# Which expert blocks' results stay on chip for the combining product: the last two, or the last one

## The reference

```
s     = sigmoid(h @ w_router)                     # 16 experts in 4 groups
idx   = top 2 experts of the best group           # by s + router_bias
gates = s[idx] / sum(s[idx])
act   = silu(h @ w_gate[e]) * (h @ w_up[e]) * gates[e]
y     = sum over e of act @ w_down[e]
x     = x + g2 * y
```

## Time and profile before

| | |
|---|---|
| median of three runs | 1651.51 us |
| the profiled execution | 1663.96 us |
| its span, first to last instruction | 1662.2 us |
| TensorE matmuls busy | 1446.6 us (87% of the span) |
| VectorE, ScalarE, GpSimd busy | 545.1, 372.3, 196.9 us |
| chain that ended last | TensorE 67%, DMA 12%, VectorE 8%, issue 5%, ScalarE 3% |
| granted TensorE clock, mean | 0.951 |
| DMA | 428.68 MB, 258 GB/s over the span |

### The profile page before, as it was taken

How to read it: one execution, slowest core, us unless ns; L and a number is a source line. 1 busy time by engine, 2 the same in 40 slices (tenths; PEclk the granted TensorE clock), 3 DMA queues, 4 the chain that set the end, 5 groups by cost and what they waited for, 6 DMA issues and landing times.

```text
span 1662.2 us, 26392 instructions
## 1 busy us (share of the span) xinstructions
PE 1446.6 (87%) x10704; PEld 857.0 (52%) x10704; DVE 545.1 (33%) x1329; ACT 372.3 (22%) x985; POOL 196.9 (12%) x286
## 2 busy tenths in 40 slices
PE   3989997998897998898989999979889899969982
PEld 1866674332676686332464456743327566843321
DVE  0126523211526625111522343332115257242114
ACT  1105421111212612111120342301102036121110
POOL 0100021101113022000110000210011000220011
PEclk9989998999999999999989999999989999979996
DMA  9996235999869126999958224379996940539992
GB/s 339 349 318 230 88 116 211 408 420 415 282 231 324 23 105 230 373 420 422 345 183 263 36 77 177 102 293 416 421 411 201 310 159 2 203 121 406 421 379 87
DMA packets 125027, 428.68 MB, mean 258 GB/s; under 512 B 13099, under 2 KB 55038, under 8 KB 100326
## 3 DMA queue, kind: packets, MB, share of 16 engines
q1 hardware_dynamic: 96854, 350.32, 54.9%
q0 software_dynamic: 21104, 72.71, 12.7%
q10 hardware_dynamic: 6944, 3.91, 0.8%
HBM read 389.20 MB, written 40.26 MB: 258 GB/s over the span
## 4 chain that ended last, share of the span: by engine, by line
PE 67%; DMA 12%; DVE 8%; issue 5%; ACT 3%; POOL 2%; another core or an unknown queue 2%; SPq 1%; DVEq 0%; ACTq 0%; POOLq 0%
PE bank L1681 59%; DMA work<-in_moe_w_gate 5%; DMA ring<-in_w_mod 4%; PE bank L1851 3%; DMA h_slots<-xn,row_of 2%; PE bank L2015 2%; ACT pp L1022 2%; PE bank L1738 1%; POOL small L698 1%; POOL h_slots L801 1%; DVE xn L1169 1%; DMA hT<-h_slots 1%; PE bank L1898 1%; SPq L606 1%
## 5 line engine op out<-in xcount | busy, mean ns | idle before, releaser
L1681 PE MATMUL bank<-ring,pp 128*32 128x512 f32 x2312 | 317.4, 597 | 14.0 <-issue 11.9
L1681 PE MATMUL bank<-ring,hT 128*128 128x256 f32 (+3 forms) x1142 | 272.2, 398 | 5.9 <-issue 3.3
L1681 PEld LDWEIGHTS bank<-ring,hT 128*128 128x128 f32 x1142 | 213.6, 196 | 62.7 <-issue 32.1
L1681 PE MATMUL bank<-work,pp 128*32 128x512 f32 x888 | 241.9, 628 | 3.0 <-DVE pp L1555 2.3
L1681 PE MATMUL bank<-ring,xn 128*128 128x256 f32 x768 | 168.2, 380 | 0.0
L1681 PEld LDWEIGHTS bank<-ring,pp 128*32 128x32 f32 x2312 | 87.4, 110 | 135.5 <-issue 134.5
L1681 PEld LDWEIGHTS bank<-ring,xn 128*128 128x128 f32 x768 | 145.0, 190 | 19.4
L1681 PE MATMUL bank<-V,pp 128*32 128x512 f32 x640 | 124.3, 634 | 30.5 <-issue 21.3
L1571 DVE TENSOR_TENSOR pp<-bank,pp 128x256 f32<-128x256 f32 x40 | 17.0, 425 | 340.1 <-ACT pp L1099 340.1
L1681 PE MATMUL bank<-ring,condT 128*32 128x256 f32 x1536 | 99.0, 404 | 17.0 <-DMA ring<-in_w_mod 17.0
L1022 ACT ACTIVATE pp<-bank,neg_max 128x384 f32<-128x384 f32 x192 | 96.7, 524 | 13.2 <-DVE neg_max L1462 10.1
(11 more groups left out here) (254 smaller groups left out, 1561.2 us busy)
## 6 DMA issues: line engine op xcount, KB each, us to landing
ring<-in_w_mod SPq DMA_DIRECT2D x96, 1024.0 KB, 8.2
ring<-in_moe_w_down SPq DMA_DIRECT2D x52, 1024.0 KB, 19.0
ring<-in_moe_w_gate SPq DMA_DIRECT2D x32, 1024.0 KB, 15.1
ring<-in_moe_w_up SPq DMA_DIRECT2D x32, 1024.0 KB, 17.5
hT<-h_slots POOLq DMA_DIRECT2D x36, 512.0 KB, 11.4
V<-in_moe_w_gate SPq DMA_DIRECT2D x16, 1024.0 KB, 13.9
V<-in_moe_w_up SPq DMA_DIRECT2D x16, 1024.0 KB, 16.3
work<-in_moe_w_gate SPq DMA_DIRECT2D x16, 1024.0 KB, 10.0
```

Source lines behind the costliest of these rows:

```text
L1681: return pe.matmul(out, lhsT, rhs, start=start, stop=stop)
```

## The change

`LATE` goes from 2 to 1. Block 8 is now stored and gathered like the eight before it, and only block 9's results are multiplied with the weighted matrix. `STORED` becomes 9, which changes the bound of the indirect loads and the weights that use it. The matrix has three squares of 128x128 instead of six, so it is turned in one go in block 4 (`LATE_PARTS` = 1), and the waits on `late_turned` and `lateT_ready` count by that. The semaphores of the stores count unevenly by parity now (five even blocks, four odd ones).

```diff
--- before.py
+++ after.py
@@ -32,7 +32,8 @@
 STARTS = [sum(SIZES[:i]) for i in range(E)]
 SLOTS = sum(SIZES)
 BLOCKS = SLOTS // P
-LATE = 2
+LATE = 1
+LATE_PARTS = -(-NB * LATE // 4)
 STORED = BLOCKS - LATE
 FURTHER = NT - NARROW
 PASSES = -(-FURTHER // P)
@@ -809,7 +810,8 @@
 
                 def stored_at(blk):
 
-                    return 16 * (STORED // 2 * L + blk // 2 + 1)
+                    each = (STORED + 1 - blk % 2) // 2
+                    return 16 * (each * L + blk // 2 + 1)
 
                 def block_out(blk):
                     pool.wait_ge(y_a, BLOCKS * L + blk + 2)
@@ -834,7 +836,7 @@
                     if blk == 2 and L < DEPTH - 1:
                         load_columns(L + 1, 0)
                 stored(STORED - 1)
-                pool.wait_ge(late_turned, 2 * (L + 1))
+                pool.wait_ge(late_turned, LATE_PARTS * (L + 1))
                 for b in range(NB):
                     for k, dst in enumerate((y_first, y_sum)):
                         nc.gpsimd.indirect_dma_start(dst[b], None, y_slots, rows_at(row_of[:, k, b:b + 1]),
@@ -1101,10 +1103,10 @@
                         turned_rows(n + 1, 1 - slot)
                     if blk > 0:
                         first_half(blk - 1)
-                    if blk in (4, 5):
+                    if 4 <= blk < 4 + LATE_PARTS:
                         i = 4 * (blk - 4)
                         w = min(4, NB * LATE - i)
-                        act.wait_ge(late_turned, 2 * L + blk - 3)
+                        act.wait_ge(late_turned, LATE_PARTS * L + blk - 3)
                         nc.scalar.copy(lateT[:, i:i + w, :], bank[3][:, 0:w * P].rearrange("p (i n) -> p i n", n=P))\
                             .then_inc(lateT_ready, 1)
                     turn_act(act, n, slot)
@@ -2097,7 +2099,7 @@
                         pe.wait_ge(late_ready, L + 1)
                         n = max(n for n in range(jobs["rank", L][0] + 1) if n % 4 == 3)
                         pe.wait_ge(freed[job_at[n][1]], job_at[n][2])
-                    pe.wait_ge(lateT_ready, 2 * L + i // 4)
+                    pe.wait_ge(lateT_ready, LATE_PARTS * L + i // 4)
                     for m in range(i, min(i + 4, NB * LATE)):
                         b, at = m // LATE, m % LATE * P
                         ins = pe.transpose(bank[3][:, (m - i) * P:(m - i + 1) * P], late[0][:, b, at:at + P], ident[:, :])
@@ -2106,13 +2108,13 @@
                 def turn_columns():
 
                     pe.wait_ge(mod_cols_in, 16 * (2 * (L + 1)))
-                    pe.wait_ge(lateT_ready, 2 * (L + 1))
+                    pe.wait_ge(lateT_ready, LATE_PARTS * (L + 1))
                     pe.transpose(bank[3][:, 256:288], m_in[:, 0, :], ident[0:32, 0:32]).then_inc(cols_turned, 1)
 
                 def add_late(b):
 
                     if b == 0:
-                        pe.wait_ge(lateT_ready, 2 * (L + 1))
+                        pe.wait_ge(lateT_ready, LATE_PARTS * (L + 1))
                         pe.wait_ge(cols_ready, min(L + 1, DEPTH - 1))
                         pe.wait_ge(act_full, BLOCKS * (L + 1) + 2)
                         pe.wait_ge(acT_ready, BLOCKS * (L + 1) + 1)
@@ -2133,10 +2135,8 @@
                         turn_rows(n + 1, 1 - slot, loaded(blk + 1))
                     if blk > 0:
                         block_down(blk - 1)
-                    if blk == 4:
-                        turn_late(0)
-                    if blk == 5:
-                        turn_late(4)
+                    if 4 <= blk < 4 + LATE_PARTS:
+                        turn_late(4 * (blk - 4))
                     if blk == 6 and L < DEPTH - 1:
                         turn_columns()
                     pe.wait_ge(act_full, n + 3)
```

## The result

The changed kernel takes 1696.77 us (median of four runs, 1694.87 to 1700.48) against 1653.72 us before (four runs, 1650.01 to 1658.09): a ratio of 1.0262, 95% interval 1.0228 to 1.0296. Slower by 43 us. The prediction was added to a median of 1651.51 us, from the three runs that stood then; a fourth of 1655.94 us moved that median up by 2.2 us. The profiled execution took 1697.12 us with a span of 1695.2 us. Against the one profile of the kernel before, whose span was 1662.2 us, that is only +33; why the two differences disagree turned out to be a finding of its own (run 9).

The account below looks back on a forecast made before the run. The prediction took two roads meeting at the first combining step as the bound, TensorE's slightly later, the gathered side with hardly any slack. 30.7 + 1.9 + 5.1 = +37.7 us on the median 1651.5 gave 1689 us, range 1670 to 1699.

Parts of the forecast that it names:

- the clock: Openings of layers 1 to 3: TensorE's stand lowers its granted clock, 2.3 + 0.5 + 2.3 = +5.1 us, between 0 and 7.
- The gate: End of each layer: block 8's store, issued only after block 8's copies, now gates all six indirect loads; the deciding term.
- The three terms of +30.7: Ends of layers 0 to 2: the next layer's scaling starts +9.9, +10.9 and +9.9 us later, together +30.7 us.
- Now two roads meet at L1166 almost together: First combining step, kernel before: block 9's copy and product against store, wait and indirect loads; TensorE's side slightly later.
- Layer 3: End of layer 3, no weights loading: store taken as 6 us, landing 5.0; +1.9 us, at the upper end +5.9.
- Removed products and turns: Six of twelve combining products a layer costed at nothing; three of six matrix turns at zero, at most 0.5 us a layer.
- Who else waits: SyncE's queue waits for ring places that VectorE frees, so later weight loads move with the layer; the shift isn't won back.
- A: Rival: store and loads land as quickly in every layer as in layer 3; +10 to +15 us, 1661 to 1666; chance 0.06.
- B: Rival: the products stay the last to come at the first combining step; about 4 us a layer, -16, 1636 us; chance 0.02.
- C: Rival: later layers win the delay back at waits for weights; +28, 1680 us, or under +8; chance 0.07.
- D: Rival: all landings at upper ends, layer 3 at +5.9, clock at 7 us; about +45, 1697 us; no separate chance.
- the lower bound: Low end of the main forecast: loads at their shortest landing, no cost of the clock; +23 us, 1675 us.

Follow-up runs that it names:

- run 9: The kernel before, unchanged, profiled once more: 1654.54 us, ratio 0.9976, profiled span 1652.1 us.
- run 10: The changed kernel, unchanged, profiled and measured again: 1696.93 us, ratio 1.0234 to the kernel before.
- run 6: The changed kernel, with SyncE's queue holding the next layer's weights until the gathered rows of b = 1 are in: 1676.82 us, ratio 1.0084.
- run 1: The kernel before, with block 8 also stored and the six indirect loads waiting for that store; twelve products kept: 1695.54 us, ratio 1.0213.
- run 5: The changed kernel, with 19 unread products added in layers 0 to 2 to keep TensorE busy through its stand: 1695.05 us, ratio 1.0174.
- run 8: The kernel before, with SyncE's queue holding the next layer's weights until the gathered rows of b = 1 are in: 1666.07 us, ratio 1.0002.
- runs 7 and 12: The changed kernel, with block 8's store issued from ScalarE's queue instead of GpSimd's, measured twice: 1691.68 us (1.0147) and 1698.09 us (1.0252).

## Why the prediction was right, point by point

1689 us was forecast and 1696.8 measured, inside the range of 1670 to 1699, with the cause that was named. Run 9 and after are the pair of profiles whose spans differ as the medians do, 1695.2 - 1652.1 = 43.1 us against 43.05:

| term | forecast | measured |
|---|---|---|
| layer 0, copy of block 8 to scaling | +9.9 | 27.80 - 17.08 = +10.7 |
| layer 1 | +10.9 | 28.79 - 15.83 = +13.0 |
| layer 2 | +9.9 | 27.99 - 16.71 = +11.3 |
| layer 3, copy of block 8 to the end | +1.9 | 46.13 - 41.45 = +4.7 |
| all between these stretches (forecast: the clock) | +5.1 | +3.5 |
| sum | +37.7 | +43.1 |

The last term is what the four stretches ahead of block 8's copies changed by: +4.3, -1.8, -2.4 and +3.4. The first of these lies ahead of any stand that the change makes, and in the other profiles that copy starts anywhere between 409.4 and 415.5. So it is scatter, and the other three sum to -0.8. They can't be told from scatter either: with run 10's profile in place of after's they sum to +10.0. The four stretches from block 8's copy repeat better, +39.6 with after's profile and +39.4 with run 10's. Of the 43 us between the medians that leaves 3.5 for all the rest, the clock included.

**The gate.** Right in place and kind. Store to first load was forecast as 10.07, 8.92 and 9.68 us and took 8.28, 8.77 and 8.85. Issue of the second load to the first combining step was forecast as 8.9, 9.5 and 9.0 and took 7.72, 8.37 and 7.85. From that step to the scaling 8.9 was forecast, 9.19, 8.88 and 8.67 came. Together the new tails were put at 30.5, 30.0 and 30.2 us, and were 27.80, 28.79 and 27.99: 6.1 us too much in all. The Trainium skill (DMA: Bandwidth & Descriptors, Anatomy of one DMA) would have 3.2 us for the store's bytes, an estimate from its figures; run 6 shows 3.75 from issue to next issue once the weights hold back, so the trace comes near it where the DMA share was 0.60, and not beside the full weight stream, where it was 8.28.

**The mis-sized term: the road that the change left.** The three terms of +30.7 subtracted as they stood, tails of 20.53, 19.00 and 20.34 us. Those held 10.3 us that a usual execution doesn't have: 7.6 of block 9's late report, and the rest in the combining products behind it, which ran at a lower clock (run 9). The 10.3 too much in the old tails less the 6.1 too much in the new ones is, within rounding, the 4.3 us by which 30.7 fell short of 35.0. The text knew that the profiled execution was 12.4 us above the median and said "I carry the difference over to the median". That step failed: the excess sat exactly in the stretches that were to be compared, and the change hides it. The marks were in the trace: a copy that started 6.76 us after the engine fell idle, released by something "remote", and the like in each layer, and TensorE's 2.73 us ahead of its products in the earlier trace rows. That 30.7 came within 4.3 us of 35.0 is in part luck, since 10.3 too much in the old tails was set off by 6.1 too much in the new ones.

**"Now two roads meet at L1166 almost together ... TensorE's side is the later one by a little."** Wrong in a usual execution: run 9 has the gathered side last by 1 us in layers 0 and 2 and TensorE's in layers 1 and 3. It made no difference to the sum, since the new store moves the gathered road past both.

**Layer 3.** +1.9 was forecast, from 13.32 us between block 8's copy and the second half's first step. In run 9 that is 8.75, and after it is 13.08: +4.3. The new side was 2.1 us too long (1631.3 - 1616.10 = 15.2 forecast, 13.08 measured), nearly all of it the store, which took 3.74 of the 6 us assumed; the combining step started 5.17 us behind the second load's issue, forecast 5.0. The old side was 4.6 too long, by the late report again. Two errors of one sign hid most of each other.

**Removed products and turns.** Costed at nothing, and run 1 agrees: with all twelve products in place the time is the same, 1.0213 (1.0167 to 1.0259).

**The clock.** The stand of 17.6 us did drop the clock, and the next turning took 0.87 us more. Against run 5 it costs 1.3, 0.5 and 2.0 us in the openings of layers 1 to 3, 3.8 together, where 2.3, 0.5 and 2.3 were forecast. So the place and the order of layers were right and the size was somewhat too large; how much of it reaches the end is open, with at most some 3.5 us left for it above and no gain in run 5's total.

**Who else waits.** As forecast, the weights moved with the layer: TensorE's wait for the modulation weights in layer 1 is 3.22 us in run 9 and 3.11 after.

**The rivals.** A was right about the mechanism if the weights were held back: run 6 against run 8 gives +10.8 us, and run 6's tails and layer 3 against run 9's +16.6; its own numbers were +10 to +15. With the weights beside it, it didn't come about, for the reason given against it, a share over 1. B fell: L1168 waits for the transfer in every layer. C isn't borne out: the total and the tails leave +3.5 us for the stretches in which something would have been won back; one layer's share can't be told from their scatter. D's +45 came near by its size, not by its causes: layer 3 reached +4.7, but the landings were shorter than forecast and the clock cost less. Its own terms add up to +47.8 (30.7, 4.2 for the longer landings, 5.9 and 7), and those of the lower bound, the shortest landing of each layer and no clock, to +30.9 and not +23; the stated bounds of +23 and +45 were both too low for the terms named with them.

## What to carry to other kernels

A product that is kept on chip may look like extra TensorE work, but what it buys is an earlier gate: here the last store ahead of a gather moved 12 to 15 us and took 11 to 13 us a layer with it where weights were loading, while the six products saved were worth nothing. Price such a change from the last producer that the gate now includes, with store and landing times of that very stretch, and if the wait can't be moved, hold back the traffic beside it: one wait on the weight queue took 15 to 20 us off again. Before subtracting a row of before, ask whether the profiled execution is a usual one: if it is off the median, look for the rows that hold the excess, above all those released by "remote", and take them out first, or take a second profile; an excess can also lie where the change doesn't reach (run 10).

## What the runs showed of the hardware

- **A late report of finished products.** In the first profile of before, block 9's copy started 6.65 to 7.85 us behind block 8's instead of 4.76, in every layer; in run 8 in two layers; in the profiles of the other eleven runs and of the changed kernel in none. In the first profile ScalarE's copy was as late. With the slower products behind it, at a mean granted clock of 0.66 over 5 us after TensorE had stood 1.93 to 3.13 us, it cost up to 3.6 us a layer. Neither GpSimd's issuing beside it (same in run 9) nor what GpSimd does next explains it. Its cause is open.
- **Transfers beside a full weight stream.** From its issue to the waiter's next issue block 8's 512 KB store took 8.0 to 8.9 us at a DMA share of 1.0 (the changed kernel and runs 5 and 10; 7.4 to 7.7 in run 1) and 3.7 to 3.8 with the stream held back (run 6); in layer 3, where no weights load, it was 3.2 to 4.7 in these kernels. From ScalarE's queue it was 7.9 to 8.8, and 3.4 in layer 3 (runs 7 and 12).
- **Chips differ for one kernel and not for another.** The kernel before took 10 us more on one chip, which was used in one session only (1666.26 against 1656 to 1658), while the kernel with ScalarE's store took 1691.68 there and 1698.09 elsewhere. The cause is open. A ratio from one chip needn't be the ratio on another: 1.0147 and 1.0252 for the same program.
